# Block sums of down weights formed by accumulating DMAs in HBM, six pairs of the last down stage as seven products, and x loaded in quarters

## The chip, the cores and the metric

One core of a Trainium2 chip runs the whole program; the other cores are idle. The metric is the device time of one launch in microseconds (us), taken as the median of several runs. The engines are named as the profile names them: PE (TensorE), ACT (ScalarE), DVE (VectorE), POOL (GpSimd), SP (SyncE, which here only issues DMAs).

## The reference

Two blocks follow each other on a sequence of 256 rows of 1024 features. The first block has depth 1, the second is applied twice. All data are float32.

```python
def first_block(x, ...):                       # DEPTH = 1
    h = rms_norm(x, norm_mix_w[layer])
    proj = h @ w_in[layer]
    ...                                        # attention o_a @ w_nsa_branch, retention o_r @ w_ret_branch
    x = x + (gate_a * y_a + gate_b * y_b) @ w_mix_out[layer]
    h = rms_norm(x, norm_ffn_w[layer])
    u = causal_dwconv(h @ w_ffn_up[layer], ffn_conv_w[layer], ffn_conv_b[layer])
    x = x + (jax.nn.silu(u_gate) * u_val) @ w_ffn_down[layer]
    return rms_norm(x, norm_final_w)

def second_block(x, ...):                      # DEPTH_2 = 2
    for l in range(DEPTH_2):
        h = rmsnorm(x, norm1_g[l])
        ...                                    # attention, convolution, fourier branch, gates
        x = x + merged @ w_out[l]
        h2 = rmsnorm(x, norm2_g[l])
        f_gate, f_up = jnp.split(h2 @ w_ffn_in[l], 2, axis=-1)
        x = x + (jax.nn.silu(f_gate) * f_up) @ w_ffn_out[l]
    return x
```

The feed forward width is 2816, so a down product has a contraction of 22 blocks of 128.

## The kernel before

**Splitting.** Every large product is made three times in the matmul's own number form: a float32 operand is split into an upper part and a rest, and upper by upper, upper by rest and rest by upper are added in PSUM (`mul3`, L559 to L561, three matmuls of 128x512).

**Chunks.** All weights stand in HBM in one array `in_w`, cut into chunks of 128x2048 float32 (1 MB). `chunk_plan` sets their order. SP loads chunk i into `raw[i % 6]` as soon as chunk i-6 is used (`load_raw`). ACT copies it into `whi[i % 4]` (the upper part, `splits`) and DVE, for some chunks POOL, writes the rest `wlo` in place of the raw data. ACT and DVE run three chunks ahead of PE (`AHEAD`). Each engine runs its own list of instructions in the order in which it is written down; only semaphores tie them. A projection of 512 columns uses a chunk for 24 matmuls (four blocks of k, two tiles of 128 tokens, three matmuls each).

**The start.** PE turns x by identity products (`first_turned`, L578, 128x128), ACT and DVE write the turned x as `hhi` and `hlo` with the first norm's gain, and the first unit `q` (chunks 0 and 1, loaded and split in quarters) is computed by `first_rows` (L721). Chunk 2 is the first of unit `kv1`, chunk 3 its second; they are loaded and split whole. Until x is there PE runs small products on a zero tile (`warm`, L696).

**The sum into x.** After a mixing stage (`to_x`, stages `mo`, `out0`, `out1`) DVE adds the four results to x (`add`, L2502), PE turns x quarter by quarter (`x_turned`), ACT and DVE write the turned quarters as `hhi` and `hlo` (`late_upper` L1386, `late_lower` L2159). POOL makes the power -1/2 for the norms (`norm_power`, L1844). For norm `n1` the result goes through two DVE copies (`late_wide`, L2169) to two PE transposes (`late_row`, L687), which stand in PE's list in the second unit of the up stage `up0`.

**The down stages.** `dn1` and `dn2` are the down products of the second block's two layers, 11 chunks each; a chunk is a pair of k blocks against 1024 columns. A plain pair is 8 block products (24 matmuls: 2 k blocks, 2 token tiles, 2 halves of the columns, three each). A pair in `SEVEN` is made in the function `seven` as 7 block products (21 matmuls): three (9 matmuls) with the chunk's own blocks, four (12 matmuls) with sums of its blocks, which stand as a chunk of their own behind it. DVE forms these sums on the chip (`weight_sums`, L2017 to L2023), from all four blocks of the chunk, and POOL forms the sums of the activations (`g_sums`). Before, pairs 1, 3, 5, 7 of both stages are of this kind:

```python
SEVEN = (1, 3, 5, 7)
```

**POOL around the change.** After the four norms of the retention and two products with `gnw` (L1894), the next instructions in POOL's list are the powers of `n1`, then the splits for `up0`.

**Compressed keys.** Units `cmpk` and `cmpv` (chunks 8 to 11, L800 and L801, 128x256, 16 matmuls a chunk) have turned pieces of the retention's queries (`ret_turned`, source `ra`) and the first layer of the hidden product between them.

Of the kernel before, what the change touches and what calls it, by code (L numbers as in the profile page):

```python
# [29 lines left out]
def chunk_plan():  # L30
# [31 lines left out]
    for l in range(2):  # L62
# [16 lines left out]
        for c in range(NFT // 2):  # L79
            halves = cols((512, 512), (0, 512)) if c in SEVEN else cols((0, 1024))  # L80
            units.setdefault(f"dn{l + 1}", []).append(len(plan))
            plan.append(("w_ffn_out_2", l, halves, 2 * c, 2))
            if c in SEVEN:
                plan.append((None, l, range(1024), 2 * c, 2))
# [3 lines left out]
SEVEN = (1, 3, 5, 7)  # L88
# [11 lines left out]
for _name, _w in SMALL:  # L100
# [6 lines left out]
    "pool_small", "d_raw0", "d_raw1", "d_raw2", "d_raw3", "d_raw4", "d_raw5", "d_x0", "d_x1", "d_small", "d_small2", "d_gain",  # L107
    "d_bias0", "d_bias1", "d_dec", "d_ctab", "d_gnw", "d_gf", "d_cs", "d_cd", "d_out",
    "d_k", "d_q0", "d_q1", "d_q2", "d_q3",
    "d_first0", "d_first1", "d_first2", "d_first3", "d_second0", "d_second1", "d_second2", "d_second3",  # L110
)
# [168 lines left out]
SUMS = {i for i in range(len(PLAN)) if PLAN[i][0] is None}  # L280

# [24 lines left out]
def place(nc, ctx):  # L306
# [78 lines left out]
    t.gsh, t.gsl = ([at(f"{w}{c}", p + o + (4, 8, 40, 30)[c], [128, 4, 128], R32) for c in range(len(SEVEN))]  # L385
# [58 lines left out]
def sp_program(sp, t, ev, d):  # L444
# [8 lines left out]
    def load_raw(i):  # L453
# [37 lines left out]
    load("d_x0", t.x[:, 0, :], d["in_x"][0:128, :], ("x", "in", 0, 0), ("x", "in", 0, 1))  # L491
    load("d_small", t.sm[:, 0:NEARLY], d["in_small"][:, 0:NEARLY], ("small",))
    for i in range(len(PLAN)):
        if i == 1:
            load("d_x1", t.x[:, 1, :], d["in_x"][128:256, :], ("x", "in", 1, 0), ("x", "in", 1, 1))
# [34 lines left out]
        if i not in SUMS:  # L530
            load_raw(i)
# [10 lines left out]
def pe_program(pe, t, ev, pb):  # L542
# [38 lines left out]
    def rows(u, hi, lo, data=()):  # L581
# [85 lines left out]
    def first_turned(tt):  # L667
        for h in range(2):
            turned(("xT", "n0", tt, h), [("x", "in", tt, h)], t.x[:, tt, half(h)], 4, 4 + 2 * tt + h)
# [31 lines left out]
    first_turned(0)  # L701
    warm(40)
# [20 lines left out]

    for kg in range(4):
# [61 lines left out]
    for kv, u in enumerate(("cmpk", "cmpv")):  # L786
# [3 lines left out]
        for c, i in enumerate(UNITS[u]):  # L790
# [255 lines left out]
    def ffn(n, norm, after):  # L1046
# [66 lines left out]
        for c in range(len(chunks) - held):  # L1113
            if n and c in SEVEN:
# [148 lines left out]
def act_program(act, t, ev, pb):  # L1263
# [103 lines left out]
    def first_upper(tt):  # L1367

        for h in range(2):
            name = ("xT", "n0", tt, h)  # L1370
            act.wait_ge(*on(*name))
            for j in range(4):
                k = 4 * h + j
                act.op.activation(t.hhi[:, k, tok(tt)], bank(name)[:, j * 128:j * 128 + 128], ACT.Copy,
                                  scale=small(t, "gain0")[:, k:k + 1]).then_inc(
                    *at("act_small", ("h hi", "n0", tt, k)))
# [25 lines left out]
    first_upper(0)  # L1402
    first_splits(0, 0, 1, 2, 3)
    norm_squares("n0", 0)
    first_splits(1, 0, 1, 2, 3)
    first_upper(1)
    splits(2)
    norm_squares("n0", 1)
    q_out = copied_rows("q", lambda tt: t.qkv[tt][:, 0:512], scale=query_scale)
    q_out(0)  # L1410
# [36 lines left out]
    for kv, u in enumerate(("cmpk", "cmpv")):  # L1447
        for c, i in enumerate(UNITS[u]):
            if kv + c < 2:
                splits(i + AHEAD)  # L1450
            if kv != c:
                ret_turned("qr", kv)
        if kv:
# [3 lines left out]
            *at("act_small", ("Hp", kv)))  # L1457
    hidden_out(1)
# [139 lines left out]
    def ffn(n, norm, after):  # L1598
# [237 lines left out]
def pool_program(pool, t, ev, pb):  # L1836
# [52 lines left out]
    for k in range(4):  # L1889
        power(("ret rs", k), st[:, 200 + 2 * k:202 + 2 * k], st[:, 192 + 2 * k:194 + 2 * k], ("ret var", k))  # L1890
        if k in (1, 2):
# [3 lines left out]
                *at("pool_small", ("sg gained", k - 1)))  # L1895
    for tt in range(2):
# [33 lines left out]
    def layer(l, norm, norm_before_ffn):  # L1930
# [27 lines left out]
        for c in SEVEN:  # L1958
            g_sums(l + 1, c)

    def g_sums(n, c):
# [6 lines left out]
        def less(dst, a, b, names=()):  # L1968
# [11 lines left out]
        pool.op.tensor_tensor(t.gsl[SEVEN.index(c)][:, :, :], t.gs[:, :, :],  # L1980
                              t.gsh[SEVEN.index(c)][:, :, :].bitcast(F32), ALU.subtract).then_inc(
# [7 lines left out]
def dve_program(dve, t, ev, pb):  # L1989
# [36 lines left out]
    def splits(last):  # L2026

        while upto[0] <= min(last, len(PLAN) - 1):
# [5 lines left out]
            if i + 1 in SUMS:  # L2034
# [106 lines left out]
    def first_lower(tt):  # L2141
        for h in range(2):
            name = ("xT", "n0", tt, h)
            dve.wait_ge(*on("h hi", "n0", tt, 4 * h + 3))
            for j in range(4):
                k = 4 * h + j
                dve.op.scalar_tensor_tensor(t.hlo[:, k, tok(tt)], bank(name)[:, j * 128:j * 128 + 128],
                                            small(t, "gain0")[:, k:k + 1], t.hhi[:, k, tok(tt)].bitcast(F32), ALU.mult,
                                            ALU.subtract).then_inc(
# [838 lines left out]
```

## Time and profile before

| | |
|---|---|
| median of 3 runs | 1247.33 us (1247.27 to 1247.52) |
| the profiled execution's own time | 1247.01 us |
| its span, first to last instruction | 1245.6 us |
| PE busy | 1239.7 us, 6640 matmuls |
| DVE, ACT, POOL busy | 957.4, 722.9, 422.0 us |
| HBM read, written | 225.31 MB, 1.05 MB |

The span is the time on the chip between the first and the last instruction. The time of the execution is 1.4 us more. Busy time of PE is the union of its matmuls; a 128x512 matmul is shown longer than the distance to the next one, since matmuls overlap, so the distance between starts is what one costs.

### The profile page before, as it was taken

How to read it: one execution, taken by the hardware profiler on the slowest of the kernel's cores; microseconds unless marked ns; L12 is line 12 of the kernel's file. 1: busy time of each engine (PE TensorE's matmuls, PEld its weight loads, DVE VectorE, ACT ScalarE, POOL GpSimd, SP SyncE). 2: the span in 40 equal slices, each digit the busy share in tenths (PEclk: the TensorE clock that was granted, in tenths of full speed). 3: DMA queues.
4: the chain of work that ended last, by engine and by line, in shares of the span. 5: the costliest groups of instructions: out<-in, count | busy, mean ns of one | idle time of the engine just before them, and what ended most of it. 6: DMA issues, size and time to landing. Idle time of an engine off the chain costs nothing.

```text
span 1245.6 us, 17081 instructions
## 1 busy us (share of the span) xinstructions
PE 1239.7 (100%) x6640; PEld 1059.7 (85%) x6640; DVE 957.4 (77%) x1374; ACT 722.9 (58%) x1020; POOL 422.0 (34%) x338
## 2 busy tenths in 40 slices
PE   9999999999999999999999999999999999999999
PEld 7988888888888889888888888888988888888887
DVE  6865668677887378986877888986898596888895
ACT  7755545377765364576836556545457674655552
POOL 0010012039892069377420112008746750011100
PEclk9999999999999999999999999999999999999999
DMA  9753334455555448744555554555855454555443
GB/s 360 261 207 136 135 119 167 172 188 200 180 193 199 173 169 256 224 153 170 180 205 179 175 198 150 186 213 189 291 174 193 158 173 165 203 178 194 156 168 115
DMA packets 38287, 233.74 MB, mean 188 GB/s; under 512 B 4672, under 2 KB 5312, under 8 KB 12224
## 3 DMA queue, kind: packets, MB, share of 16 engines
q1 hardware_dynamic: 38208, 232.67, 53.7%
q8 instruction: 52, 0.85, 0.3%
q14 instruction: 27, 0.22, 0.0%
HBM read 225.31 MB, written 1.05 MB: 182 GB/s over the span
## 4 chain that ended last, share of the span: by engine, by line
PE 97%; DVE 1%; DMA 1%; ACT 1%; SPq 0%; issue 0%; DVEq 0%; ACTq 0%
PE ps L652 19%; PE ps L559 18%; PE ps L561 18%; PE ps L560 18%; PE ps L657 10%; PE ps L564 6%; PE ps L578 2%; PE ps L619 1%; PE ps L620 1%; PE ps L618 1%; DMA raw<-in_w 1%; PE ps L1199 1%; SPq L451 0%; PE ps L883 0%; DVE wlo L2039 0%; ACT whi L1289 0%
## 5 line engine op out<-in xcount | busy, mean ns | idle before, releaser
L1289 ACT ACTIVATE whi<-raw 128x2048 fp32r<-128x2048 f32 (+1 forms) x213 | 401.5, 1890 | 115.3 <-PE ps L561 101.5
L2039 DVE TENSOR_TENSOR wlo<-raw,whi 128x2048 fp32r<-128x2048 f32 (+2 forms) x169 | 390.3, 2315 | 89.7 <-ACT whi L1289 88.7
L1872 POOL TENSOR_TENSOR wlo<-raw,whi 128x512 fp32r<-128x512 f32 x176 | 229.1, 1337 | 88.6 <-ACT whi L1289 85.5
L652 PE MATMUL ps<-hh,whi 128*128 128x512 f32 x1056 | 255.8, 391 | 0.0
L652 PEld LDWEIGHTS ps<-hh,whi 128*128 128x128 f32 x1056 | 193.0, 188 | 36.5
L559 PE MATMUL ps<-whi,hh 128*128 128x512 f32 (+1 forms) x504 | 201.4, 400 | 0.1
L561 PE MATMUL ps<-whi,hh 128*128 128x512 f32 (+1 forms) x504 | 195.4, 388 | 0.0
L560 PE MATMUL ps<-wlo,hh 128*128 128x512 f32 (+1 forms) x504 | 195.2, 387 | 0.0
L1844 POOL TENSOR_TENSOR st<-st,sm 128x1 f32<-128x1 f32 (+2 forms) x28 | 45.9, 1640 | 392.9 <-DVE st L2093 220.4
L657 PEld LDWEIGHTS ps<-hh,wlo 128*128 128x128 f32 x1056 | 137.7, 191 | 6.7
L657 PE MATMUL ps<-hh,wlo 128*128 128x256 f32 x1056 | 139.7, 282 | 0.0
L561 PEld LDWEIGHTS ps<-whi,hh 128*128 128x128 f32 x504 | 94.6, 188 | 20.0
L559 PEld LDWEIGHTS ps<-whi,hh 128*128 128x128 f32 x504 | 95.0, 189 | 18.0 <-DVE wlo L2039 0.9
L560 PEld LDWEIGHTS ps<-wlo,hh 128*128 128x128 f32 x504 | 95.0, 188 | 16.7 <-issue 0.5
L2686 DVE SCALAR_TENSOR_TENSOR ps<-gp,sm,ps 128x256 f32<-128x256 f32 x232 | 99.4, 483 | 0.0
L559 PE MATMUL ps<-whi,ghi 128*128 128x512 f32 x224 | 87.3, 390 | 0.0
L560 PE MATMUL ps<-wlo,ghi 128*128 128x512 f32 x224 | 87.2, 389 | 0.0
L561 PE MATMUL ps<-whi,glo 128*128 128x512 f32 x224 | 87.2, 389 | 0.0
L1635 ACT ACTIVATE fu<-ps 128x512 f32<-128x512 f32 x44 | 26.3, 599 | 101.5 <-PE ps L657 101.5
L1980 POOL TENSOR_TENSOR gsl<-gs,gsh 128x512 fp32r<-128x512 f32 x8 | 18.6, 2329 | 104.1 <-ACT gsh L1337 104.1
L2543 DVE SCALAR_TENSOR_TENSOR fu<-ps,sm,fu 128x255 f32<-128x255 f32 (+1 forms) x88 | 38.3, 476 | 16.6 <-ACT fu L1626 15.9
L561 PEld LDWEIGHTS ps<-whi,glo 128*128 128x128 f32 x224 | 42.1, 188 | 8.8
(348 smaller groups left out, 2053.1 us busy)
## 6 DMA issues: line engine op xcount, KB each, us to landing
raw<-in_w SPq DMA_DIRECT2D x203, 1024.0 KB, 4.9
gain<-in_bias SPq DMA_DIRECT2D x12, 256.0 KB, 5.2
raw<-in_w SPq DMA_DIRECT2D x8, 256.0 KB, 6.7
kst<-kh SPq DMA_DIRECT2D x16, 128.0 KB, 2.8
qst<-qh SPq DMA_DIRECT2D x16, 128.0 KB, 2.3
raw<-in_w SPq DMA_DIRECT2D x2, 560.0 KB, 13.0
x<-in_x SPq DMA_DIRECT2D x2, 512.0 KB, 5.4
gain<-in_rows SPq DMA_DIRECT2D x2, 512.0 KB, 5.8
```

What stands on the lines that cost most here:

```text
L559: pe.op.matmul(o, sh, mh, start=start, stop=False, skip_group_check=True)
L560: pe.op.matmul(o, sh, ml, start=False, stop=False, skip_group_check=True)
L561: signalled(pe.op.matmul(o, sl, mh, start=False, stop=stop, skip_group_check=True), names)
L564: signalled(pe.op.matmul(o, a, b, start=start, stop=stop, skip_group_check=True), names, "pe_small")
L652: pe.op.matmul(o[:, :], wh[:, k, c], t.hh[:, k, :, :], start=k == 0, stop=False, skip_group_check=True)
L657: ins = pe.op.matmul(o[:, 0:S], wl[:, k, c], t.hhi[:, k, :], start=False, stop=k == 7, skip_group_check=True)
L1289: act.op.activation(t.whi[i % NHI][:, c], t.raw[i % NRAW][:, c], ACT.Copy).then_inc(*at("act_hi", ("hi", i)))
L1844: pool.op.tensor_tensor(o, a, small(t, "mhalf")[:, 0:a.shape[-1]], ALU.pow).then_inc(*at("pool_small", name))
L1872: pool.op.tensor_tensor(t.wlo[i % NRAW][:, half(k)], t.raw[i % NRAW][:, half(k)], t.whi[i % NHI][:, half(k)].bitcast(F32), ALU.subtract).t ...
L2039: dve.op.tensor_tensor(t.wlo[i % NRAW][:, c], t.raw[i % NRAW][:, c], t.whi[i % NHI][:, c].bitcast(F32), ALU.subtract).then_inc(*at("dve_lo ...
L2543: dve.op.scalar_tensor_tensor(u[:, v, j:S], bank(name)[:, 0:S - j], fc[:, f, v, 2 - j:3 - j], u[:, v, j:S], ALU.mult, ALU.add).then_inc(*a ...
L2686: ins = dve.op.scalar_tensor_tensor(t.cv[:, f, :] if j == 30 else acc, t.gp[:, f, j:j + S], cw[:, f, j:j + 1], acc, ALU.mult, ALU.add)
```

## The change

The change has five parts.

1. `SEVEN` becomes one tuple for each of the two layers: pairs 1, 2, 4, 5 in `dn1` (four as before, other ones) and 1, 2, 4, 5, 6, 7 in `dn2` (six).
2. DVE forms the sums for pair 4 alone in each stage. For the other eight pairs the sums stand in a new HBM array `sums` of eight chunks. SP copies blocks of the weights there, HBM to HBM, two DMAs of 512 KB ahead of each of the loads of chunks 18 to 25. POOL then issues 32 accumulating DMAs of 256 KB in three dependent rounds (16, 8, 8), with a wait for the landing of the round before; they stand between the retention's powers and the powers of `n1`. The chunk itself is then loaded without its first block (768 KB), and its sums are loaded as a chunk of 1 MB.
3. At the start, `small` is loaded first and x in four quarters; chunk 2 is loaded and split in quarters too. Turning x, its `hhi` and `hlo` and the products of unit `q` are ordered by quarters. The squares of the first norm come behind the splits of chunk 2.
4. In `to_x` DVE adds the second half of token tile 0 to x before `late_lower` of tile 1, and the last quarter before `late_lower(0, 1)`.
5. The turned piece `qr` of token tile 1 moves behind the last chunk of `cmpv`.

```diff
-SEVEN = (1, 3, 5, 7)
+SEVEN = ((1, 2, 4, 5), (1, 2, 4, 5, 6, 7))
+BY_DVE = ((4,), (4,))
...
+FORMED = [i for i in sorted(SUMS) if PLAN[i][3] // 2 not in BY_DVE[PLAN[i][1]]]
+COPIES = range(18, 18 + len(FORMED))
...
-        if i < 2:
+        if i < 3:
             for k in range(4):
-                load(f"d_{('first', 'second')[i]}{k}", t.raw[i][:, half(k)], src[:, half(k)], ("raw", i, k))
+                load(f"d_{('first', 'second', 'third')[i]}{k}", t.raw[i][:, half(k)], src[:, half(k)], ("raw", i, k))
             return
-        load(f"d_raw{i % NRAW}", t.raw[i % NRAW][:, 0:width(i)], src, ("raw", i))
+        c = slice(512 if i + 1 in FORMED else 0, width(i))
+        load(f"d_raw{i % NRAW}", t.raw[i % NRAW][:, c], src[:, c], ("raw", i))
+
+    def load_sums(i):
+        sp.wait_ge(*on("used", i - NRAW))
+        sp.wait_ge(*on("sums formed"))
+        load(f"d_raw{i % NRAW}", t.raw[i % NRAW][:, :], d["sums"][FORMED.index(i)], ("raw", i))
+
+    def blocks_copied(n):
...
+        for h in range(2):
+            load("d_copied", d["sums"][n][:, 1024 * h:1024 * h + 1024], src[:, 512 + 512 * h:1536 + 512 * h],
...
+        if i in COPIES:
+            blocks_copied(i - COPIES[0])
...
-    first_turned(0)
-    warm(40)
+    first_turned(0, 0)
+    warm(34)
...
-            if kv != c:
+            if c:
                 ret_turned("qr", kv)
-            if kv == 1 and c == 0:
+            elif kv:
                 hidden(0)
...
+    def sums_formed():
...
+        def added(sem, dst, src, *names):
+            pool.op.dma_start(dst, src, accum_op=ALU.add).then_inc(*at(sem, *names, by=16))
+
+        last = FORMED[-1]
+        pool.wait_ge(*on("blocks copied"))
+        for n, i in enumerate(FORMED):
+            first = d["in_w"][offs[i - 1]:offs[i]].rearrange("(p n) -> p n", p=128)[:, 0:512]
+            for j in range(2):
+                added("d_one", d["sums"][n][:, half(j)], first, *([("first sums",)] * (j and i == last)))
+        pool.wait_ge(*on("first sums"))
+        for n, i in enumerate(FORMED):
+            added("d_two", d["sums"][n][:, half(2)], d["sums"][n][:, half(0)], *([("second sums",)] * (i == last)))
+        pool.wait_ge(*on("second sums"))
+        for n, i in enumerate(FORMED):
+            added("d_three", d["sums"][n][:, half(3)], d["sums"][n][:, half(2)], *([("sums formed",)] * (i == last)))
...
+    sums_formed()
     for tt in range(2):
         norm_power("n1", tt)
...
-            if i + 1 in SUMS:
+            if i + 1 in SUMS and i + 1 not in FORMED:
                 weight_sums(i)
...
         late_lower(norm, 0, 0)
+        add(0, 1)
         late_lower(norm, 1, 0)
-        add(0, 1)
         splits(chunks[2] + AHEAD)
         norm_mean(norm, 0)
+        add(1, 1)
         late_lower(norm, 0, 1)
-        add(1, 1)
         late_lower(norm, 1, 1)
```

**ACT and DVE at the start.** The first rows are DVE's list from the program's begin, before the change: `hh` is the turned x, L2008 a quarter's rest of chunk 0 or 1, L2039 a whole chunk's.

```order
2 L2147 SCALAR_TENSOR_TENSOR hh<-ps,sm,hh 128x128 x8
3 L2008 TENSOR_TENSOR wlo_55<-raw_49,whi_61 128x512 x4
4 L2093 TENSOR_SCALAR st<-st 128x1
5 L2008 TENSOR_TENSOR wlo_56<-raw_50,whi_62 128x512 x4
6 L2147 SCALAR_TENSOR_TENSOR hh<-ps,sm,hh 128x128 x8
7 L2039 TENSOR_TENSOR wlo_57<-raw_51,whi_63 128x2048
```

The same place after the change, on ACT, whose list now has the same pattern (L1406 writes the turned x, L1309 the quarters, L1378 the squares, L1322 whole chunks).

```order
1 L1406 ACTIVATE hh<-ps,sm 128x128 x4
2 L1309 ACTIVATE whi_61<-raw_49 128x512 x4
3 L1406 ACTIVATE hh<-ps,sm 128x128 x8
4 L1309 ACTIVATE whi_62<-raw_50 128x512 x4
5 L1406 ACTIVATE hh<-ps,sm 128x128 x4
6 L1309 ACTIVATE whi_63<-raw_51 128x512 x4
7 L1378 ACTIVATE xn_72,st<-x 128x512 x2
8 L1378 ACTIVATE xn_73,st<-x 128x512 x2
9 L1322 ACTIVATE whi_64<-raw_52 128x2048
```

The turned x no longer comes eight tiles at a time; four come ahead of chunk 0, and chunk 2 is four quarters with the squares behind them and ahead of chunk 3.

**DVE in the sum into x of stage `mo`.** Before the change:

```order
208 L2502 TENSOR_TENSOR x<-ps,x 128x512 x2
209 L2159 SCALAR_TENSOR_TENSOR hh<-ps,sm,hh 128x128 x8
210 L2502 TENSOR_TENSOR x<-ps,x 128x512
211 L2039 TENSOR_TENSOR wlo_60<-raw_54,whi_62 128x2048
212 L2093 TENSOR_SCALAR st<-st 128x1
213 L2159 SCALAR_TENSOR_TENSOR hh<-ps,sm,hh 128x128 x4
214 L2502 TENSOR_TENSOR x<-ps,x 128x512
```

And with the change:

```order
207 L2563 TENSOR_TENSOR x<-ps,x 128x512 x2
208 L2218 SCALAR_TENSOR_TENSOR hh<-ps,sm,hh 128x128 x4
209 L2563 TENSOR_TENSOR x<-ps,x 128x512
210 L2218 SCALAR_TENSOR_TENSOR hh<-ps,sm,hh 128x128 x4
211 L2099 TENSOR_TENSOR wlo_60<-raw_54,whi_62 128x2048
212 L2153 TENSOR_SCALAR st<-st 128x1
213 L2563 TENSOR_TENSOR x<-ps,x 128x512
214 L2218 SCALAR_TENSOR_TENSOR hh<-ps,sm,hh 128x128 x8
```

The third addition has moved ahead of four of the eight tiles of `hh`, and the fourth ahead of the next four.

**POOL between retention and up stage.** Before the change, L1894 is the product with `gnw` and L1844 a power:

```order
19 L1844 TENSOR_TENSOR st<-st,sm 128x2
20 L1894 TENSOR_TENSOR sg<-sg,gnw 128x1024
21 L1844 TENSOR_TENSOR st<-st,sm 128x2
22 L1844 TENSOR_TENSOR st<-st,sm 128x1 x2
23 L1872 TENSOR_TENSOR wlo_56<-raw_50,whi_64 128x512 x4
```

With the change:

```order
19 L1880 TENSOR_TENSOR st<-st,sm 128x2
20 L1953 TENSOR_TENSOR sg<-sg,gnw 128x1024
21 L1880 TENSOR_TENSOR st<-st,sm 128x2
22 L1921 DMA sums<-in_w 128x512 x16
23 L1921 DMA sums<-sums 128x512 x16
24 L1880 TENSOR_TENSOR st<-st,sm 128x1 x2
25 L1908 TENSOR_TENSOR wlo_56<-raw_50,whi_64 128x512 x4
```

32 DMAs stand between the last power of the retention and the two powers of `n1`.

## Rows read from the trace of the kernel before

**Rows 1.** The page: PE's busy time, granted clock, and shares of the chain.

```profile
PE 1239.7 (100%) x6640; PEld 1059.7 (85%) x6640; DVE 957.4 (77%) x1374; ACT 722.9 (58%) x1020; POOL 422.0 (34%) x338
...
PEclk9999999999999999999999999999999999999999
...
PE 97%; DVE 1%; DMA 1%; ACT 1%; SPq 0%; issue 0%; DVEq 0%; ACTq 0%
```

**Rows 2.** PE's waits: line, for whom, us in total, times, longest.

```profile
PE ps L578 <- DVE x L2502: 0.7, 3, 0.2
PE ps L578 <- DVE ra L2270: 0.3, 1, 0.3
```

**Rows 3.** Timeline of PE in unit kv1: start, duration, instruction; six matmuls apart.

```profile
24.03 0.39 PE L559 MATMUL ps<-whi,hh 128*128 128x512 f32 x1
...
25.39 0.39 PE L559 MATMUL ps<-whi,hh 128*128 128x512 f32 x1
```

**Rows 4.** Timeline of the first 24 us, with idle time before in brackets.

```profile
4.83 1.09 PE L578 MATMUL ps<-sm,x 128*128 128x128 f32 x8 [0.79 <-DMA sm<-in_small]
...
5.52 2.18 ACT L1374 ACTIVATE hh<-ps,sm 128x128 fp32r<-128x128 f32 x8 [3.52 <-PE ps L578]
...
7.54 2.35 ACT L1276 ACTIVATE whi<-raw 128x512 fp32r<-128x512 f32 x4
...
8.36 1.22 PE L721 MATMUL ps<-whi,hh 128*128 128x512 f32 x4 [0.21 <-ACT whi L1276]
...
23.92 2.29 DVE L2039 TENSOR_TENSOR wlo<-raw,whi 128x2048 fp32r<-128x2048 f32 x1 [0.98 <-ACT whi L1289]
```

**Rows 5.** The chain that ended last, first 24 us: start, us, what.

```profile
6.90 9.87 DMA raw<-in_w
...
16.79 1.93 ACT whi L1289
...
18.81 2.30 DVE wlo L2039
...
21.16 0.50 PE ps L559
```

**Rows 6.** Busy time by stretch (us; x instructions), granted clock, DMA share, GB/s.

```profile
8.36:21.16 12.80, 12.70 (x57) 9.47 (x57) 10.15 (x22) 10.48 (x24) 0.55 (x1) 1.00 1.02 405
...
70.00:125.00 55.00, 55.00 (x282) 45.49 (x281) 36.57 (x48) 26.88 (x52) 4.57 (x2) 1.00 0.44 153
196.00:268.00 72.00, 71.76 (x347) 59.75 (x347) 48.89 (x60) 40.16 (x52) 1.41 (x4) 1.00 0.52 183
```

**Rows 7.** Timeline of PE between the chunks of cmpv.

```profile
59.00 0.44 PE L578 MATMUL ps<-sm,ra 128*128 128x128 f32 x2 [0.30 <-DVE ra L2270]
```

**Rows 8.** Timeline of DVE in stage mo, then of PE in stage out0.

```profile
253.05 1.13 DVE L2159 SCALAR_TENSOR_TENSOR hh<-ps,sm,hh 128x128 fp32r<-128x128 f32 x4 [1.67 <-ACT hh L1386]
256.20 1.13 DVE L2159 SCALAR_TENSOR_TENSOR hh<-ps,sm,hh 128x128 fp32r<-128x128 f32 x4 [2.02 <-ACT hh L1386]
...
659.47 0.39 PE L561 MATMUL ps<-whi,ml 128*128 128x512 f32 x1
660.10 0.66 PE L578 MATMUL ps<-sm,x 128*128 128x128 f32 x4 [0.24 <-DVE x L2502]
```

**Rows 9.** Timelines of POOL, DVE and PE from the retention to the up stage.

```profile
193.39 2.68 POOL L1844 TENSOR_TENSOR st<-st,sm 128x2 f32<-128x2 f32 x1 [1.26 <-DVE st L2423]
...
267.21 0.55 POOL L1844 TENSOR_TENSOR st<-st,sm 128x1 f32<-128x1 f32 x1 [6.09 <-DVE st L2093]
267.73 5.05 POOL L1872 TENSOR_TENSOR wlo<-raw,whi 128x512 fp32r<-128x512 f32 x4
...
267.80 1.31 DVE L2169 COPY xn<-st 128x128 f32<-128x128 f32 x1 [0.53 <-POOL st L1844]
...
270.12 0.38 PE L687 MATMUL ps<-sm,xn 128*128 128x128 f32 x2
```

**Rows 10.** DMA issues: KB each, median us from issue to landing.

```profile
kst<-kh SPq DMA_DIRECT2D x16, 128.0 KB, 2.8
```

More of the change, by code:

```diff
@@ L1365, in norm_upper, with first_upper @@
                   bank(name)[:, :].rearrange("p (k s) -> p k s", k=4), name)
[L1367 to L1376, printed above, removed]
+    def first_upper(tt, h):
+        name = ("xT", "n0", tt, h)
+        act.wait_ge(*on(*name))
+        for j in range(4):
+            k = 4 * h + j
+            act.op.activation(t.hhi[:, k, tok(tt)], bank(name)[:, j * 128:j * 128 + 128], ACT.Copy,
+                              scale=small(t, "gain0")[:, k:k + 1]).then_inc(
+                *at("act_small", ("h hi", "n0", tt, k)))
     def late_upper(norm, tt, h):
@@ L1399, in heads_upper @@
                       bank((name, tt, g))[:, :].rearrange("p (k s) -> p k s", k=4), (name, tt, g))
-    first_upper(0)
+    first_upper(0, 0)
     first_splits(0, 0, 1, 2, 3)
-    norm_squares("n0", 0)
+    first_upper(1, 0)
+    first_upper(0, 1)
     first_splits(1, 0, 1, 2, 3)
-    first_upper(1)
-    splits(2)
-    norm_squares("n0", 1)
+    first_upper(1, 1)
+    first_splits(2, 0, 1, 2, 3)
+    for tt in range(2):
+        norm_squares("n0", tt)
     q_out = copied_rows("q", lambda tt: t.qkv[tt][:, 0:512], scale=query_scale)
+    splits(3)
     q_out(0)
@@ L1450, in act_program @@
                 splits(i + AHEAD)
-            if kv != c:
-                ret_turned("qr", kv)
+            if c and not kv:
+                ret_turned("qr", 0)
         if kv:
@@ L2139, in norm_lower, with first_lower @@
                   bank(name)[:, :].rearrange("p (k s) -> p k s", k=4), t.hhi[:, blk, tok(tt)], ("h hi", norm, tt, h))
[L2141 to L2149, printed above, removed]
-                    *at("dve_out", ("h k", "n0", tt, k), *([("h", "n0", tt, h), ("free", name)] if j == 3 else [])))
+    def first_lower(tt, h):
+        name = ("xT", "n0", tt, h)
+        dve.wait_ge(*on("h hi", "n0", tt, 4 * h + 3))
+        for j in range(4):
+            k = 4 * h + j
+            dve.op.scalar_tensor_tensor(t.hlo[:, k, tok(tt)], bank(name)[:, j * 128:j * 128 + 128],
+                                        small(t, "gain0")[:, k:k + 1], t.hhi[:, k, tok(tt)].bitcast(F32), ALU.mult,
+                                        ALU.subtract).then_inc(
+                *at("dve_out", ("h k", "n0", tt, k), *([("h", "n0", tt, h), ("free", name)] if j == 3 else [])))
     def late_lower(norm, tt, h):
@@ L2184, in dve_program @@
                          ALU.add).then_inc(*at("dve_small", ("sel",)))
-    first_lower(0)
+    first_lower(0, 0)
     first_splits(0, 0, 1, 2, 3)
-    norm_mean("n0", 0)
+    first_lower(1, 0)
+    first_lower(0, 1)
     first_splits(1, 0, 1, 2, 3)
-    first_lower(1)
-    splits(2)
-    norm_mean("n0", 1)
+    first_lower(1, 1)
+    first_splits(2, 0, 1, 2, 3)
+    for tt in range(2):
+        norm_mean("n0", tt)
     def rs_eighth(tt):
```

82 lines of the change are left out of this document (50 added, 32 removed).

## The prediction, made before the changed kernel was run

> **What bounds the kernel now.** I read the page first: PE is busy for 1239.7 of the 1245.6 us at the full granted clock, and the chain that ended last is PE for 97% [rows 1]. So time is won only by fewer matmuls, by ending one of PE's few gaps, or by starting earlier; and it is lost as soon as some other engine or a DMA is late by more than its slack. The timeline gives the price of a matmul: six of 128x512 start 1.36 us apart, 0.227 us each, though each is drawn 0.39 long [rows 3]. PE's waits name two kinds of gap inside the program: three times the addition to x (L2502) and once the rotated queries `ra` [rows 2]. The rest of the lost time is at the start. There the chain runs over the landing of chunk 2 at 16.77, ACT's 1.93 and DVE's 2.30 us on it to PE's first product of `kv1` at 21.16 [rows 5], and the DMA engines are full from 8.36 to 21.16 at 405 GB/s [rows 6].
>
> **The change part by part.**
>
> *Two more pairs as seven products.* 24 matmuls become 21 in two pairs of `dn2`: 2 x 3 x 0.227 = 1.4 us [rows 3]. In `dn1` four pairs stay four, so nothing. PE is bound here, so this counts in full if the feed holds. A formed pair takes 21 x 0.227 = 4.8 us on PE. ACT and DVE split 1536 and 2048 columns, 1.75 times 1.93 and 2.30 = 3.4 and 4.0 us [rows 5]; DVE's sums fall away in all but pair 4, so both fit. The loads are 1.84 MB, which at 405 GB/s take 4.5 us [rows 6]. All three are under 4.8, so I cost the feed at nothing; at 352 GB/s (the 183 GB/s at share 0.52 scaled up [rows 6]) it is 5.2 us, 0.4 too much in each of three pairs in a row, 1.2 us at most. Two more `g_sums` on POOL are hidden: POOL works 422 us in all [rows 1].
>
> *The additions to x.* PE's last matmul before x's second half starts at 659.47 and the next at 660.10, 0.63 us for what costs 0.227: 0.40 lost, and the page of waits has it three times, 1.2 us in all [rows 2, 8]. In stage `mo` the four copies ahead end at 253.05 + 1.13 = 254.2 and the next four start at 256.20, because ACT's are late [rows 8]; the addition (under 0.7) now fits in that hole. I take the whole 1.2 us; at least 0 if its sum were not ready by then.
>
> *The piece `qr` of tile 1.* PE idled 0.30 us for DVE [rows 7]; it now asks 16 matmuls later, and nothing behind it is short. I take 0.3.
>
> *The start.* Before, 620 KB land ahead of the first turn at 4.83 [rows 4]; now 364 KB, so at 405 GB/s 0.6 us earlier, 4.2. ACT begins 0.7 later (5.52 against 4.83) and writes four tiles (2.18/8 = 0.27 each) instead of eight: 6.0; its first quarter takes 0.59, and PE's first product is at about 6.8 instead of 8.36 [rows 4]. That lead is not kept. ACT then has, up to the end of its split of chunk 3, 16 tiles of x (4.4), 12 quarters at 0.59 (7.1), four squares (2.5, estimated as four splits of 512 columns) and 1.93: 15.9 us without a wait. From 4.9 that is 20.8; with an estimated 0.9 us for the landing of chunk 0's last quarter and 1.5 for PE's turn of the next quarter of x it is 23.2, and DVE's 2.3 behind it end at 25.6. Before, that split ended at 23.92 + 2.29 = 26.2, and PE wanted it at 21.16 + 24 x 0.227 = 26.6 [rows 3 to 5]. So `kv1` can begin at about 20, but its second chunk holds PE to 25.6: I take 1.0 us. The ends: 0 if ACT is later by one more such wait, and 3.0 if DMA alone sets it (16.77 + 1.05 MB at 405 GB/s = 2.6, + 1.93 + 2.30 = 23.6 against 26.6).
>
> *The copies.* 8.4 MB go from HBM to HBM between 70 and 125 us, where the DMA engines are used to 0.44 at 153 GB/s [rows 6]. Doubling that fills them to 0.88. They are issued behind a load and ahead of the wait for the next one, so they run in the gap. Cost 0; if the gap were missing, 2.6 us a load, but six buffers cover it.
>
> *The accumulating DMAs.* This is the term that decides. POOL is free at 193.39 + 2.68 = 196.07. Its next duty, the second power of `n1`, runs at 267.21 and DVE's copy of it ends at 269.1; PE wants it at 270.12 [rows 9]. So 1.0 us is spare, and with two powers of 0.55 POOL must be through at 267.7: 71.6 us. Within them lie two whole rounds with their landings and the issue of the third. Added are 4.2 MB and then 2.1 MB, 6.3 MB. The landings cost twice about 2.8 us (a small DMA from issue to landing [rows 10]). No issue of a DMA by POOL stands in the trace; it is bounded by nothing and by the 5.05 us that POOL needs for four operations of 128x512, and I take one of those, 1.26 us, eight times: 10.1 [rows 9]. That leaves 55.9 us for 6.3 MB, so the point from which it decides is 113 GB/s. The rate is bounded by the free share in this stretch: 0.48 of 352 GB/s is 169 if an added byte costs the engines what a loaded one costs, 85 if it costs double, since the destination is read as well [rows 6]. I take 120, just under the middle: 52 us, done at 264, with 3.5 us to spare and no stall. At 169 there are 19 us to spare; at 85 it takes 74 us and PE stalls 18.
>
> On this the Trainium skill speaks against the change. "Collectives: The Full Stack", section "Why ReduceScatter is half of AllGather", says that the adder in the DMA costs no cycles, but that the second source halves the rate. By that rule it would be the 85 GB/s of the last sentence but three and a stall; no run here shows it yet. "SBUF — State Buffer" has a box on DMAs issued from the POOL queue, whose descriptors are held up by some DVE operations; it would raise the 1.26 us and push the same way.
>
> *Sum.* 1.4 + 1.2 + 0.3 + 1.0 = 3.9 us. The profiled execution took 1247.01; 1243.1. The median is 0.3 above that execution, so 1243.4 us.
>
> **The rivals.**
>
> *The accumulating DMAs are late (slower).* At 85 GB/s POOL comes 18 us late to `n1`, PE stands before its two transposes in the second unit of `up0`, and what was won is lost: 1243.4 + 18 = 1261 us. For it: the margin is only 3.5 of 71.6 us, and DVE is busy 49 of the 72 us in the stretch [rows 6], beside POOL's issuing. Against it: the engines have 0.48 of their time free. A lateness of 1.5 to 6 us would bring it to between -0.2% and +0.2%. Chance 0.27 for late by over 6 us, 0.06 for less.
>
> *The loads suffer from them.* PE takes 1.05 MB every 5.45 us here, 192 GB/s. If POOL's DMAs got half of the engines, the loads would keep 176 GB/s of 352, and each chunk would take 0.5 us more than PE's; over 13 chunks 6.5 us, of which six buffers swallow one chunk's 5 us. Some 1.5 to 3 us are lost, 1245.5. Chance 0.05.
>
> *The feed of the last down stage is short.* 1.2 us as above: 1244.6, faster still. Chance 0.04.
>
> **How the numbers follow.** The forecast as it stands has 0.58, with a range of its own from 1241.5 (start worth 3) to 1244.8 (start worth nothing and a wait left). 0.2% is 2.5 us and is about what can be told from no change. Faster: 0.58 and the feed's 0.04, 0.62. Within 0.2%: the small lateness and part of the loads', 0.09. Slower: 0.27 and the rest, 0.29. For 8 in 10 the range must reach into the late case: up to 1260.
>
> **What would show it.** Right: 6 matmuls fewer of 128x512 in `dn2`; no wait of PE on L2563; `kv1`'s first product near 20 us; the third round's last issue before about 265 us and the powers of `n1` on POOL where they were, less the lead; PE's transposes in `up0` without a gap. Wrong: a gap of PE ahead of those transposes with POOL as the releaser, or ACT waiting for `raw` between 200 and 280 us, or gaps with DMA as the releaser in the last down stage.

## The result, and the profile after

The changed kernel takes 1256.29 us (median of 5 runs, 1255.15 to 1259.96) against 1247.33 us before (5 runs, 1246.94 to 1247.54): ratio 1.0076, 95% interval 1.0065 to 1.0086. It is 9 us slower, where 4 us faster was forecast. The profiled execution is the longest of the five, 1259.96 us with a span of 1258.0; the spans of the others are 1253.1 to 1254.7, so what follows for that one execution is up to 5 us more than a typical one loses.

The page after, to be read against that of before [rows 1]. PE has 12 matmuls fewer (6 of them are fewer of the small ones that keep it busy at the start), its share of the span is 99% where it was 100%, and the chain of work that ended last, PE for 97% of the span before, is now PE for 91% and DMA for 6%:

```profile
span 1258.0 us, 17140 instructions
PE 1239.7 (99%) x6628; PEld 1060.5 (84%) x6628; DVE 953.2 (76%) x1361; ACT 726.8 (58%) x1027; POOL 459.5 (37%) x380
PEclk9999999989999999999999999999999999999999
DMA  9797338995555537764455554664864454555474
PE 91%; DMA 6%; POOL 2%; DVE 1%; ACT 0%; issue 0%; SPq 0%; DVEq 0%
```

The ninth slice (252 to 283 us) has the one lower digit of the clock. PE's waits name the place; the two kinds of wait inside the program that stood in [rows 2] are gone, and one of 12.8 us is new, with a small one of 0.3:

```profile
PE ps L714 <- DVE xn L2228: 12.8, 1, 12.8
PE ps L748 <- ACT whi L1309: 1.1, 2, 0.7
PE ps L723 <- POOL zero L1892: 1.0, 1, 1.0
PE ps L587 <- DVE wlo L2099: 0.3, 1, 0.3
```

L714 is the pair of transposes in the second unit of `up0`, for which [rows 9] has DVE's copy and POOL's power one behind the other. The timeline of POOL from the retention on (start, us, what; in brackets the idle time before and its releaser):

```profile
192.22 2.68 POOL L1880 TENSOR_TENSOR st<-st,sm 128x2 f32<-128x2 f32 x1 [1.25 <-DVE st L2484]
194.85 13.61 POOL L1921 DMA_DIRECT2D sums<-in_w  x16
247.06 6.69 POOL L1921 DMA_DIRECT2D sums<-sums  x8 [38.60 <-DMA sums<-in_w]
269.81 6.70 POOL L1921 DMA_DIRECT2D sums<-sums  x8 [16.06 <-DMA sums<-sums]
274.02 3.62 POOL L1880 TENSOR_TENSOR st<-st,sm 128x1 f32<-128x1 f32 x2
275.10 7.40 POOL L1908 TENSOR_TENSOR wlo<-raw,whi 128x512 fp32r<-128x512 f32 x4
```

The same stretch on DVE and PE:

```profile
265.32 0.21 DVE L2153 TENSOR_SCALAR st<-st 128x1 f32<-128x1 f32 x1
277.14 4.24 DVE L2228 COPY xn<-st 128x128 f32<-128x128 f32 x2 [11.61 <-POOL st L1880]
281.30 0.69 DVE L2614 TENSOR_TENSOR ps<-ps,us 128x512 f32<-128x512 f32 x1
281.52 0.66 PE L714 MATMUL ps<-sm,xn 128*128 128x128 f32 x2 [12.84 <-DVE xn L2228]
```

Round 1 (16 DMAs) is issued at 194.85 and has landed by 247.0, 52.2 us for 4.2 MB or 80 GB/s; round 2 runs from 247.06 to 269.8, 22.8 us for 2.1 MB or 92 GB/s. By then PE has been out of work since 268.7. What follows stands in a row: POOL's issue of round 3 to 276.5, the two powers to 277.6, two copies on DVE to 281.4. Busy time by stretch (us; engines; granted clock, DMA share, GB/s):

```profile
194.85:247.00 52.15, 52.15 (x247) 43.47 (x247) 35.00 (x34) 27.04 (x23) 13.61 (x17) 1.00 0.99 261
269.80:276.00 6.20, 0.00 (x0) 0.00 (x0) 0.00 (x0) 0.00 (x0) 6.19 (x11) 0.78 0.92 198
276.00:286.00 10.00, 4.47 (x14) 3.83 (x15) 8.13 (x7) 1.41 (x3) 6.50 (x7) 0.50 0.93 168
```

The DMA engines, 0.52 used in this stretch before [rows 6], are full for all of it. And in the gap the granted clock falls to 0.50, the 1.2 GHz level, and stays there until some 5 us after PE has work again.

By the starts of PE's stages the 12.4 us between the two profiled spans come from here:

| stage | before | after | difference |
|---|---|---|---|
| `kv1` begins | 21.16 | 20.64 | -0.5 |
| `up0` begins | 261.22 | 259.62 | -1.1 more |
| `up0` lasts | 121.1 | 136.6 | +15.5 |
| end of `up0` to begin of `up2` | 679.9 | 679.0 | -0.9 |
| last down stage | 59.06 | 58.33 | -0.7 |

The 15.5 us of `up0` are 13.0 of gap and 2.5 of the lower clock behind it. Everything else came out as a gain, 3.2 us together.

### The profile page after: what moved, and what is told of

Read it like the earlier page. It is cut to its first block, busy times and chain, and to the rows that moved or that the text cites. A ratio compares the mean times of both kernels' runs of the same rounds, so it can differ in the third digit from the quotient of the medians.

```text
span 1258.0 us, 17140 instructions
## 1 busy us (share of the span) xinstructions
PE 1239.7 (99%) x6628; PEld 1060.5 (84%) x6628; DVE 953.2 (76%) x1361; ACT 726.8 (58%) x1027; POOL 459.5 (37%) x380
## 4 chain that ended last, share of the span: by engine, by line
PE 91%; DMA 6%; POOL 2%; DVE 1%; ACT 0%; issue 0%; SPq 0%; DVEq 0%
PE ps L680 19%; PE ps L587 16%; PE ps L589 16%; PE ps L588 16%; PE ps L685 10%; PE ps L592 6%; DMA sums<-in_w 3%; PE ps L606 2%; DMA sums<-sums 1%; POOL sums L1921 1%; PE ps L648 1%; PE ps L647 1%; PE ps L646 1%; PE ps L748 1%; DMA raw<-sums 1%; PE ps L1232 1%
## 5 line engine op out<-in xcount | busy, mean ns | idle before, releaser
L1322 ACT ACTIVATE whi<-raw 128x2048 fp32r<-128x2048 f32 (+1 forms) x214 | 403.1, 1888 | 117.7 <-PE ps L589 93.8
L2099 DVE TENSOR_TENSOR wlo<-raw,whi 128x2048 fp32r<-128x2048 f32 (+1 forms) x170 | 391.7, 2312 | 94.9 <-ACT whi L1322 94.2
L1880 POOL TENSOR_TENSOR st<-st,sm 128x1 f32<-128x1 f32 (+2 forms) x28 | 48.7, 1829 | 342.8 <-DVE st L2153 179.3
L587 PE MATMUL ps<-whi,ghi 128*128 128x512 f32 x214 | 83.5, 390 | 0.0
L588 PE MATMUL ps<-wlo,ghi 128*128 128x512 f32 x214 | 83.3, 389 | 0.0
L589 PE MATMUL ps<-whi,glo 128*128 128x512 f32 x214 | 83.3, 389 | 0.0
L2040 POOL TENSOR_TENSOR gsl<-gs,gsh 128x512 fp32r<-128x512 f32 x10 | 23.3, 2330 | 89.1 <-ACT gsh L1370 89.1
## 6 DMA issues: line engine op xcount, KB each, us to landing
sums<-sums POOLq DMA_DIRECT2D x16, 256.0 KB, 10.4
```

The lines of the kernel that those rows point to most:

```text
L587: pe.op.matmul(o, sh, mh, start=start, stop=False, skip_group_check=True)
L588: pe.op.matmul(o, sh, ml, start=False, stop=False, skip_group_check=True)
L589: signalled(pe.op.matmul(o, sl, mh, start=False, stop=stop, skip_group_check=True), names)
L1322: act.op.activation(t.whi[i % NHI][:, c], t.raw[i % NRAW][:, c], ACT.Copy).then_inc(*at("act_hi", ("hi", i)))
L1880: pool.op.tensor_tensor(o, a, small(t, "mhalf")[:, 0:a.shape[-1]], ALU.pow).then_inc(*at("pool_small", name))
L2099: dve.op.tensor_tensor(t.wlo[i % NRAW][:, c], t.raw[i % NRAW][:, c], t.whi[i % NHI][:, c].bitcast(F32), ALU.subtract).then_inc(*at("dve_lo ...
```

## The experiments

Each time stands beside runs of the kernel before on the same chip. "The late variant" is the second experiment.

**The change without its sums in HBM.**

```diff
-SEVEN = ((1, 2, 4, 5), (1, 2, 4, 5, 6, 7))
-BY_DVE = ((4,), (4,))
+SEVEN = ((1, 3, 5, 7), (1, 3, 5, 7))
+BY_DVE = SEVEN
...
-    sums_formed()
```

> The changed kernel without its block sums in HBM: pairs 1, 3, 5, 7 in both last down stages and DVE's sums as before, no copies, no accumulating DMAs; only the quarters at the start, the order of the additions to x and the moved piece qr stay. Theory (the loss is POOL's wait for the rounds, the small edits do gain): in the changed kernel's trace the start is 0.5 to 0.7 us earlier, up0 begins 1.6 us earlier and each of the two later additions gains 0.45, so 2.5 us below the kernel before, about 1244.8 us, and no gap before the transposes in up0. Rival (the small edits gain nothing by themselves, their lead is given back): 1247.3, ratio 1.000.

Measured: 1244.14 us against 1247.16, ratio 0.9975 (0.9965 to 0.9984). The start, the additions and the moved `qr` are worth 3.0 us. By stages: `kv1` begins 1.2 us earlier (19.91), the stretch to `up0` is 1.1 us shorter, and each of the two later stages `out` gives 0.4 us; the last down stage lasts 59.06 us as before.

**The late variant: round 1 in its place, rounds 2 and 3 behind `up0`.**

```diff
-    sums_formed()
+    sums_formed(1)
...
+    sums_formed(2, 3)
     start("n3", 0)
```

> The changed kernel with rounds two and three of the accumulating DMAs moved in POOL's list behind the loop of up0, ahead of the first power of n3; round one stays. Theory (PE's gap is POOL standing at the landing of rounds one and two): POOL's list reaches the powers of n1 in time, the gap of 13.0 us and the matmuls at half clock behind it are gone, 3.2 us below the kernel before, about 1244.1. Rival (the accumulating DMAs cost by taking the DMA engines from the weight loads): the loads of 200 to 250 us still land late, PE gets gaps with wlo or whi as releaser there or in the first down stage, 1247 or more.

Measured: 1243.96 us, ratio 0.9976 (0.9967 to 0.9985). POOL's timeline has the powers of `n1` in time:

```profile
193.83 13.64 POOL L1921 DMA_DIRECT2D sums<-in_w  x16
258.39 0.58 POOL L1880 TENSOR_TENSOR st<-st,sm 128x1 f32<-128x1 f32 x1 [50.92 <-DVE st L2157]
264.60 0.55 POOL L1880 TENSOR_TENSOR st<-st,sm 128x1 f32<-128x1 f32 x1 [5.63 <-DVE st L2157]
```

Round 1 still lands only at 243.7; nobody waits for it. So it is the place of the waits that costs, not the traffic. But PE's waits show what ate the two pairs' 1.4 us:

```profile
PE ps L587 <- DVE wlo L2103: 1.5, 1, 1.5
```

It stands at 1220.5 ahead of the sums of pair 7 in the last down stage, whose load took 8.7 us from issue (1207.4) to landing (1216.1); the stage lasts 59.6 us.

**The rounds alone, on the kernel before; their result is not used.**

```diff
+        if i in COPIES:
+            blocks_copied(i - COPIES[0])
...
+    sp.wait_ge(*on("sums formed"))
     sp.wait_ge(*ev.mine("d_out"))
...
+    sums_formed()
     for tt in range(2):
         norm_power("n1", tt)
```

> The kernel before with only the copies and the three rounds of accumulating DMAs added at the places where the change has them; their result is not used, SP waits for the third round at the very end. Theory: the whole loss is there, 13 us of a gap and 2.5 us at the lower clock in the profile, as in the changed kernel: 1247.3 + 12 to 16 = 1259 to 1263, since nothing is won beside it. Rival (the loss needs the other edits, for instance the loads of the sums): 1247 to 1250.

Measured: 1263.01 us, ratio 1.0128 (1.0115 to 1.0142), 16 us slower with nothing else changed. `up0` lasts 136.9 us, and PE's wait is the same one:

```profile
PE ps L701 <- DVE xn L2207: 13.5, 1, 13.5
```

**The same 32 DMAs as plain copies.** The block sums are then not formed, and the down stages use the copied blocks in their stead.

```diff
-            pool.op.dma_start(dst, src, accum_op=ALU.add).then_inc(*at(sem, *names, by=16))
+            pool.op.dma_start(dst, src).then_inc(*at(sem, *names, by=16))
```

> The changed kernel with the 32 DMAs of the three rounds as plain copies of the same bytes, same places and waits; the block sums are therefore not formed, all else is. It prices the addition itself. Theory A (an added byte costs the engines double, since the destination is read too): round one, 52.2 us with additions at 80 GB/s, takes about 26 to 32 us, rounds one and two end before 245, no gap of PE, about 1244 us. Theory B (these DMAs are slow for their 2 KB rows or their issue from POOL, not for the addition): round one stays over 45 us and most of the gap stays, over 1250 us.

Measured: 1243.41 us, ratio 0.997 (0.9958 to 0.9981), no gap in `up0`. POOL's timeline, and the busy time of round 1:

```profile
194.40 8.51 POOL L1921 DMA_DIRECT2D sums<-in_w  x16
225.95 4.13 POOL L1921 DMA_DIRECT2D sums<-sums  x8 [23.05 <-DMA sums<-in_w]
239.45 4.14 POOL L1921 DMA_DIRECT2D sums<-sums  x8 [9.37 <-DMA sums<-sums]
```

```profile
194.40:225.70 31.30, 31.30 (x148) 26.14 (x147) 22.67 (x22) 18.69 (x16) 8.50 (x17) 1.00 0.94 311
```

The rounds take 31.6 and 13.5 us, 133 and 155 GB/s, in place of 52.2 and 22.8: the addition makes the same bytes 1.65 to 1.7 times as long. That is against the changed kernel's longest execution; against the same rounds in other traces (49.8 to 50.2 us, and 20.5 to 20.9) it is 1.5 to 1.6 times.

What a byte costs in engine time is read from the shares of the two DMA queues. Each line gives packets, MB and the share of the 16 engines; q0 is POOL's queue and q1 is SP's. First the changed kernel between 200 and 245 us, then the plain copies between 200 and 225 us:

```profile
q0 software_dynamic: 2207, 4.00, 56.7%
q1 hardware_dynamic: 1068, 7.83, 46.0%
```

```profile
q0 software_dynamic: 1158, 3.77, 52.0%
q1 hardware_dynamic: 575, 4.22, 45.1%
```

MB divided by time and share is the rate that each kind would have with all engines to itself: 157 GB/s for the additions and 378 for the loads beside them, 290 for the copies and 374 for the loads beside those. So an added byte costs 2.4 times as much as a loaded one (2.2 times by the 352 GB/s of the kernel before [rows 6]), a copied one 1.3 times, and the addition alone makes 1.85 of it. The last down stage had no gap in this run and lasts 57.7 us: the two pairs are worth 1.36 us where their loads come in time.

**Round 1 early, in POOL's idle stretch behind the rotation of `kr`.**

```diff
+    sums_formed(1)
     for k in range(4):
         power(("ret rs", k)
...
-    sums_formed()
+    sums_formed(2, 3)
```

> As after, but round 1 of the accumulating DMAs (16 of 256 KB) stands on POOL right behind the rotation of `kr`, in the idle stretch before the retention's powers; rounds 2 and 3 stay where the change put them. Theory (only the rates decide, the rounds are late because 4.2 MB at 80 and 2.1 MB at 92 GB/s do not fit between 196 and 268 us): round 1 starts when the copies have landed, near 117 us, and takes 35 to 52 us, so it is done by 170; round 2 starts near 195 and takes 23 us, round 3 is issued by 225, PE has no gap in `up0`, and the time is that of the late variant, 1243.4 to 1244.0 us. Rival (the place costs: DMA engines are fuller in this stretch and the loads of the gates and the heads come late): new gaps of PE between 117 and 170 us, 1245 or more. Rival (POOL is held by its issues and the retention's powers come late): a gap of PE behind POOL near 190, over 1250.

Measured: 1244.62 us (8 runs, 1243.01 to 1245.45), ratio 0.9976 (0.9966 to 0.9986). POOL's timeline:

```profile
117.39 13.64 POOL L1921 DMA_DIRECT2D sums<-in_w  x16 [38.19 <-DMA sums<-in_w]
...
194.26 6.75 POOL L1921 DMA_DIRECT2D sums<-sums  x8
216.57 6.69 POOL L1921 DMA_DIRECT2D sums<-sums  x8 [15.56 <-DMA sums<-sums]
258.82 0.57 POOL L1880 TENSOR_TENSOR st<-st,sm 128x1 f32<-128x1 f32 x1 [35.55 <-DVE st L2157]
```

Round 1 has landed at 159.4, after 42.0 us (100 GB/s, beside fewer loads), and no gap appeared, in this stretch or in `up0`. The rivals fell. The median lies 0.6 us above the forecast; the profiled execution (span 1241.5) doesn't show why.

**Five sums in HBM, `dn1`'s all on DVE.**

```diff
-BY_DVE = ((4,), (4,))
+BY_DVE = ((1, 2, 4, 5), (4,))
```

> As after, but DVE forms the sums of all four pairs of `dn1`, as before the change, and only five sums of `dn2` are formed in HBM, all rounds at the place of the change. Theory (duration goes by bytes): round 1 adds 2.6 MB in 33 us, round 2 1.3 MB in 14 us, so the powers of `n1` are asked for at about 245 us, 20 us ahead of their need: no gap in `up0`, 1243.4 to 1244.0 us. Rival (a fixed time for each round, or DVE's work in `up0` and not bytes sets it): round 1 stays above 45 us, and a gap of some us stays.

Measured: 1243.57 us, ratio 0.9972 (0.9961 to 0.9983). The rounds take 33.6 and 16.7 us (78 and 78 GB/s), against the 33 and 14 expected. Round 1 goes by bytes (the full one ran at 80 to 84 GB/s); round 2 is 2.7 us longer than expected, and what holds it no trace shows. Neither is near the 45 us of the rival. POOL is through at 248.9, 10 us before DVE asks for the first power. What 0.8 us of gap in the last down stage takes back here, pair 7 again, the next experiment is about.

**The late variant, with pair 7 of the last down stage on DVE too.**

```diff
-BY_DVE = ((4,), (4,))
+BY_DVE = ((4,), (4, 7))
```

> As the late variant, but DVE forms the sums of pair 7 of `dn2` too, so the 1 MB load of that pair's sums falls away from the burst of pairs 5 to 7, whose late landing left PE a gap of 1.7 us. Theory (that gap is the feed: loads of 1.84 MB for every 4.8 us of PE): no gap in the last down stage, which takes 57.7 us instead of 59.6, 1242.3 us. Rival (DVE is then late with pair 7, or the gap moves to pair 6): a gap of 0.5 to 2 us stays, 1243 to 1244 us.

Measured: 1242.62 us (1242.21 to 1243.22), ratio 0.9963 (0.9951 to 0.9976), the fastest of all. PE's waits, all of them:

```profile
PE ps L723 <- POOL zero L1892: 1.0, 1, 1.0
PE ps L748 <- ACT whi L1309: 0.2, 1, 0.2
```

The gap is gone and the stage lasts 57.8 us; DVE had room for the sums. That the gap came from the feed by DMA is shown by the late landing above. That one load less ends it is likely, but not shown by this trace alone: the plain copies, round 1 early and the eight DMAs below keep the load of pair 7's sums and have no such gap in their profiled executions either, and the two ratios' intervals overlap (0.9951 to 0.9976 here, 0.9967 to 0.9985 for the late variant). The stronger sign is that all five runs lie within 1.0 us, where the eleven of the late variant spread over 4.0.

**Rows of 4 KB in round 1.** Eight DMAs of 128x1024 in place of 16 of 128x512; the source is the first 1024 columns, so the sums are other numbers.

```diff
-            first = d["in_w"][offs[i - 1]:offs[i]].rearrange("(p n) -> p n", p=128)[:, 0:512]
-            for j in range(2):
-                added("d_one", d["sums"][n][:, half(j)], first, *([("first sums",)] * (j and i == last)))
+            first = d["in_w"][offs[i - 1]:offs[i]].rearrange("(p n) -> p n", p=128)[:, 0:1024]
+            added("d_one", d["sums"][n][:, 0:1024], first, *([("first sums",)] * (i == last)))
```

> As after, but round 1 is made of 8 DMAs of 128x1024 instead of 16 of 128x512 (rows of 4 KB in place of 2 KB). The source is then the first 1024 columns in place of the first 512 twice, so the block sums, and with them the results of the down stages, are other numbers; the bytes added are the same 4.2 MB. Theory (bytes set the rate): round 1 takes 52 us again and the gap of 13 us stays, 1256 us. Rival (a cost for each row or packet sets it): round 1 takes 30 to 40 us, and the gap is gone or short, 1244 to 1247 us.

Measured: 1248.97 us, ratio 1.0016 (1.0006 to 1.0025), between the two. Round 1 took 43.1 us (97 GB/s) for the same bytes, and the wait shrank to 3.0 us:

```profile
237.49 6.70 POOL L1921 DMA_DIRECT2D sums<-sums  x8 [36.21 <-DMA sums<-in_w]
```

```profile
PE ps L714 <- DVE xn L2227: 3.0, 1, 3.0
```

Neither theory had it alone. Bytes don't set the rate by themselves. Three things differ from the changed kernel: the rows are longer, the DMAs are fewer, and each byte of the source is read once and not twice. The next experiment holds the rows and halves the DMAs.

**Eight DMAs in round 1, rows of 2 KB.**

```diff
-            first = d["in_w"][offs[i - 1]:offs[i]].rearrange("(p n) -> p n", p=128)[:, 0:512]
-            for j in range(2):
-                added("d_one", d["sums"][n][:, half(j)], first, *([("first sums",)] * (j and i == last)))
+            first = d["in_w"][offs[i - 1]:offs[i]].rearrange("(p one n) -> p one n", p=128, one=1)[:, :, 0:512]
+            added("d_one", d["sums"][n][:, 0:1024].rearrange("p (j n) -> p j n", j=2), first.to_broadcast([128, 2, 512]),
+                  *([("first sums",)] * (i == last)))
```

> As after, but round 1 is made of 8 DMAs instead of 16: one for each sum, which reads the first block twice (a repeated dimension of the source) and adds it to 128x2x512 of the destination. Rows stay 2 KB, bytes stay 4.2 MB; only the number of DMAs halves. With rows of 4 KB the same round took 43.1 us in place of 52.2. Theory (the length of the rows made that difference): round 1 takes 52 us again, the gap of 13 us stays, 1256 us. Rival (the number of DMAs made it): round 1 takes 43 us, the gap is 3 us, 1249 us.

Measured: 1254.63 us, ratio 1.0069 (1.0052 to 1.0086). Round 1 takes 50.2 us, round 2 20.9, the wait is 9.0 us:

```profile
244.57 6.74 POOL L1921 DMA_DIRECT2D sums<-sums  x8 [40.67 <-DMA sums<-in_w]
```

That is 2 us less than in the changed kernel's profiled execution and within what the same round varies by: with its 16 DMAs untouched it took 49.8 us in the late variant, 50.0 in the experiment below, 52.2 in the changed kernel and 53.4 on the kernel before. So the number of DMAs is not it. What is left is the length of the rows and the second reading of the source, and no experiment parts these two. The shares of POOL's queue don't part them clearly either: with all engines to themselves, the additions of round 1 in rows of 2 KB would run at 148 to 165 GB/s in the traces that have them, those of rounds 2 and 3, which read their source once in rows of 2 KB, at 149 to 180, and round 1 in rows of 4 KB at 183. This execution is also what a typical one of the changed kernel looks like: a gap of 9 us, a span of 1253.1.

**Round 3 behind the powers of `n1`.**

```diff
-    sums_formed()
+    sums_formed(1, 2)
     for tt in range(2):
         norm_power("n1", tt)
+    sums_formed(3)
```

> As after, but round 3 stands on POOL behind the two powers of `n1` instead of ahead of them; rounds 1 and 2 are untouched. Theory (the loss is POOL's wait for the landing of round 2, near 269, which stands ahead of the powers, and not the bytes in flight): POOL is at the powers when DVE asks (258 and 265 us), PE has no gap in `up0` and keeps its full clock, though the rounds land as late as before; POOL's first splits of `up0` come some 3 us late and are swallowed; 1243.4 to 1244.5 us. Rival (POOL's splits of `up0` are then late): a gap of PE of 1 to 4 us near 275 us, 1245 to 1248 us.

Measured: 1245.12 us (10 runs, 1243.16 to 1247.15), ratio 0.9985 (0.9976 to 0.9994). The big gap is gone and the clock stays, but a gap of 1.8 us stands at 282.1, as the rival said in size, though not by its mechanism. PE's wait, and the timelines of POOL and of DVE:

```profile
PE ps L680 <- DVE fu L2608: 1.6, 1, 1.6
```

```profile
265.67 6.74 POOL L1921 DMA_DIRECT2D sums<-sums  x8
269.96 14.52 POOL L1908 TENSOR_TENSOR wlo<-raw,whi 128x512 fp32r<-128x512 f32 x8
```

```profile
269.57 12.56 DVE L2103 TENSOR_TENSOR wlo<-raw,whi 128x2048 fp32r<-128x2048 f32 x1
282.06 1.77 DVE L2608 SCALAR_TENSOR_TENSOR fu<-ps,sm,fu 128x255 f32<-128x255 f32 x4
```

POOL's issue held its splits back until eight of them stood in a row. Beside them one split of DVE, 2.3 us when alone, lasted 12.56 us, and `fu` behind it was late for PE. It was DVE that was held up. One part of this stays open: the split begins at 269.57, POOL's issue lasts to 272.4, and in round 1 splits of DVE beside the issue took their usual 2.29 us; why this one was not done by 272.4 no trace shows.

## Why the prediction was wrong

**The step that failed** is "I take 120, just under the middle", the rate of the accumulating DMAs. In the prediction's own terms, issue and landings counted apart, the first two rounds ran at 91 GB/s: from POOL's start at 194.85 to the end of round 3's issue at 276.5 it is 81.7 us, less 6.7 for the issue and the two landings of 2.8. The deciding point was 113. I had two ends, 85 and 169, from one question, whether an added byte costs the engines once or twice, and chose between them by the middle. The traces answer it: 2.2 to 2.4 times (the queues' shares in the experiment with plain copies), so the lower end was the value. A middle of two mechanisms is no mechanism. The rule that stood in the prediction against the change, of the Trainium skill's "Collectives: The Full Stack" (section "Why ReduceScatter is half of AllGather"), agrees with that: the second source halves the rate, and plain copies in the same place were 1.5 to 1.7 times as fast in time and 1.85 times in engine time.

**The other terms of that sum.** The issue was sized 1.26 us for each DMA from another operation; it is 6.7 us for eight, 0.84 each, 3.4 us less than I took. The rival "the accumulating DMAs are late" named the mechanism, the place and the waiting transposes, and at 85 GB/s had POOL 18 us late; POOL was 10.4 us late: 276.5 against 267.7 less the 1.6 us by which all of it stood earlier. PE's gap is larger than POOL's lateness by the two copies on DVE: before, the first was done early and the second took 1.31 us [rows 9]; now both are left to the end and take 4.24 us beside POOL's splits, 2.9 more. 10.4 and 2.9 make 13.3, for a gap of 13.0. What the rival lacked is the clock: after 13 us without work PE ran at 1.2 GHz for a while, 2.5 us more. The chance of 0.27 for this case was too low: only the choice of rate stood against it. The box in the Trainium skill's "SBUF — State Buffer" that would have raised the issue's price is about operations of DVE in its two-port mode, such as a copy of fp32 within SBUF. DVE ran no such copy beside the issue of round 1, so no run here tests it; with DVE's splits and products beside it POOL issued its 16 DMAs at an even 0.84 us each.

**Two more pairs, 1.4 us:** right in size, 1.36 where no gap follows (plain copies, and the eight DMAs in round 1) and 1.3 with pair 7 on DVE. In the changed kernel 0.73, since the feed of pair 7 came late by 0.5 us; in the late variant 1.7 us late, and the whole gain gone. "I cost the feed at nothing" was thus wrong by up to 1.7 us, above the 1.2 that the rival gave it. The load of pair 7's sums took 8.7 us to land in the one execution and 4.7 in another with the same order and bytes, so the margin of 0.3 us for each pair, worked out from the mean rate, was no margin.

**The additions to x, 1.2 us, and `qr`, 0.3:** right. [Rows 2] has four such waits and the changed kernel none; 0.4 us for each later stage by the table of stages, and 1.1 us for the stretch with one addition and `qr`, somewhat more than the 0.7 asked for; where the other 0.4 comes from is open.

**The start, 1.0 us:** 0.5 in the changed kernel's profiled execution, 1.2 without the sums, 0.9 to 1.5 in the other eight kernels that have the new start. The reason given for the small value, that ACT's split of chunk 3 holds PE, did not show: `kv1`'s second chunk follows without a wait in every trace. So the size is right by luck. PE's first product came at 6.6 (6.8 forecast), and what holds PE from there is the landing of chunk 0's quarters: in the kernel without the sums in HBM the second lands at 6.7, ACT splits it, PE goes on at 7.50 and then works without a break. In the changed kernel PE waits 1.1 us for these splits in place of 0.4, which is the 0.7 us between the two.

**The copies, nothing, and the loads beside the rounds:** right. The stretch from `kv1` to `up0` got shorter, not longer, with 8.4 MB copied in it. In the rounds the loads landed 9.1 us after their issue instead of 4.8, and PE waited for none of them.

What stays open: why the same round takes 50 to 53 us from one execution to another; whether the longer rows or the single reading of the source made the round with 4 KB faster; and why DVE's split was held before POOL's splits could run.

## What to carry to other kernels

An accumulating DMA from HBM to HBM, in rows of 2 KB, is priced by the engine time left over, and each added byte takes more than twice that of a loaded one: count free share times peak rate, then halve it. Its waits matter more than its bytes: the same rounds made the kernel 12 us longer where POOL had a duty behind them than where it had none (1256.3 against 1244.0). And a stall that is paid once in the middle of a kernel is paid again at the engine that must catch up: here in DVE's copies (2.9 us) and in PE's clock (2.5 us). When a term decides the verdict and its two ends come from two mechanisms, measure which one holds before choosing a value: here the rounds alone would have told.

## What the runs showed of the hardware

- Accumulating DMAs, HBM to HBM, beside loads of some 180 GB/s: round 1 in rows of 2 KB at 78 to 84 GB/s, in rows of 4 KB at 97, and at 100 beside fewer loads. Rounds 2 and 3, whose source and destination are both `sums`, ran at 78 to 102 while PE worked, and round 3 at 118 to 132 in the three traces in which PE stood still for half of it or more and few loads ran. Plain copies of the same blocks: 133 to 155.
- POOL's issue of a DMA: 0.84 us with the addition and 0.52 us without. In the trace the issues start 0.52 apart and their ends 0.84 apart, so what stands behind them on POOL is drawn with a start before it runs: the two powers at 274.02 end at 277.1 and 277.6.
- A DVE split (two inputs in SBUF, 128x2048) that met eight POOL splits in a row took 12.56 us instead of 2.29; it ended 2.2 us after the sixth of them, and the seventh was then the one that waited. Where it meets the last of a row of four it takes 3.3. The Trainium skill's "SBUF — State Buffer" (section "Who interferes with whom") describes an exclusive lock between the two for such operations, by which the later one waits for the whole of the earlier. The trace agrees in kind, and shows six splits of POOL passing before DVE's was done; it does not explain the first 2.8 us of DVE's wait, in which POOL was still issuing.
- A gap of 3.1 us brought PE's granted clock to 0.66 on the mean of the 5 us behind it and cost 1.6 us more; gaps of 9 us (eight DMAs in round 1) and 13 us (the changed kernel) cost 2.5 us each, and the one of 13.7 us in the rounds alone 2.1.
